# Experts stage: tokens and the list of indices read from PSUM, and the gathered rows spread anew

## What is computed

```python
q = (hb @ wq).reshape(128, 8, 2, 128)            # 8 heads, two halves
s = einsum('thsd,snd->thsn', q, subkeys)         # 128 keys for each half
s1, i1 = top_k(s[:, :, 0], 16);  s2, i2 = top_k(s[:, :, 1], 16)
sc, ci = top_k(s1[..., :, None] + s2[..., None, :], 16)
idx  = e1 * 128 + e2                             # of 16384 experts
gate = softmax(sc)
act  = gelu(einsum('td,thkd->thk', hb, u_tab[idx])) * gate
out  = einsum('thk,thkd->td', act, v_tab[idx])   # 128 choices for each token
```

## Time and profile before

| what | value |
|---|---|
| median of 3 runs | 4457.77 us (4456.28 to 4461.15) |
| span of the profiled execution | 4448.2 us |
| choice of the experts, units 0 to 75 | about 1027 to 1376 us |
| gates | about 1376 to 1638 us |
| last 14 units of the first table | to about 1702 us |
| second table | to about 2240 us |
| PE, DVE, ACT, POOL busy over the span | 95%, 70%, 41%, 35% |

### The profile page before, as it was taken

One profiled execution on the slowest core, in us unless ns is written; L12 is line 12 of the kernel. 1 busy time (PEld: TensorE's weight loads), 2 busy tenths in 40 slices (PEclk: granted clock), 3 DMA queues, 4 the chain that ended last, 5 costly groups with the idle time before them and its releaser, 6 DMA issues.

```text
span 4448.2 us, 66516 instructions
## 1 busy us (share of the span) xinstructions
PE 4243.8 (95%) x26227; PEld 3699.9 (83%) x26227; DVE 3101.9 (70%) x4740; ACT 1806.5 (41%) x2814; POOL 1550.2 (35%) x1005
## 2 busy tenths in 40 slices
PE   7979989999989999999999999999999999999998
PEld 5857745779989999999989877699889877877997
DVE  5866667559878988788878555588478544555873
ACT  4245411233334544333345335455255333323542
POOL 2044224215887657777721110211111110112121
PEclk8989999999999999999999999999999999999999
DMA  4133522224875779999933322133323332102332
GB/s 180 53 105 124 182 69 70 80 89 157 260 247 199 271 287 393 376 382 388 366 108 105 95 87 66 48 105 96 100 91 105 95 104 77 47 34 68 103 99 75
DMA packets 232190, 665.74 MB, mean 150 GB/s; under 512 B 22519, under 2 KB 88455, under 8 KB 229704
## 3 DMA queue, kind: packets, MB, share of 16 engines
q1 hardware_dynamic: 110528, 389.87, 26.1%
q0 software_dynamic: 38752, 142.90, 8.8%
q10 hardware_dynamic: 82600, 128.71, 8.1%
HBM read 593.24 MB, written 68.16 MB: 149 GB/s over the span
## 4 chain that ended last, share of the span: by engine, by line
PE 74%; DVE 16%; POOL 3%; ACT 3%; issue 3%; DMA 1%; ACTq 0%; DVEq 0%; POOLq 0%
PE ps L271 14%; PE ps L272 14%; PE ps L273 14%; PE ps L2727 5%; PE ps L2729 5%; PE ps L2728 5%; DVE r L240 2%; PE ps L1611 2%; DVE A L2042 2%; PE ps L3762 1%; PE ps L1690 1%; DVE A L2341 1%; POOL r L240 1%; DVE A L2342 1%; DVE r L290 1%
## 5 line engine op out<-in xcount | busy, mean ns | idle before, releaser
L271 PE MATMUL ps<-r,r 128*128 128x384 f32 (+1 forms) x3944 | 1454.4, 369 | 22.2 <-POOL r L240 14.6
L272 PE MATMUL ps<-r,r 128*128 128x384 f32 (+1 forms) x3944 | 1436.3, 364 | 0.0
L273 PE MATMUL ps<-r,r 128*128 128x384 f32 (+1 forms) x3944 | 1435.8, 364 | 0.0
L240 DVE TENSOR_TENSOR r<-A,r 128x1024 fp32r<-128x1024 f32 x436 | 603.9, 1387 | 718.7 <-ACT r L234 713.0
L234 ACT ACTIVATE r<-A 128x1024 fp32r<-128x1024 f32 x513 | 542.2, 1058 | 1200.9 <-PE ps L273 995.3
L271 PEld LDWEIGHTS ps<-r,r 128*128 128x128 f32 x3944 | 745.6, 189 | 118.7 <-issue 24.5
L272 PEld LDWEIGHTS ps<-r,r 128*128 128x128 f32 x3944 | 745.7, 189 | 81.5 <-issue 3.4
L273 PEld LDWEIGHTS ps<-r,r 128*128 128x128 f32 x3944 | 745.2, 189 | 81.6
L287 ACT ACTIVATE r<-A 128x512 fp32r<-128x512 f32 (+1 forms) x796 | 474.1, 611 | 503.4 <-DVE A L2415 233.5
L2727 PE MATMUL ps<-r,r 128*128 128x256 f32 x2128 | 601.0, 282 | 3.5 <-DVE A L2891 2.5
L2729 PE MATMUL ps<-r,r 128*128 128x256 f32 x2128 | 600.4, 282 | 0.0
(11 more groups left out here) (532 smaller groups left out, 5544.8 us busy)
## 6 DMA issues: line engine op xcount, KB each, us to landing
A<-in_pu SPq DMA_DIRECT2D x128, 512.0 KB
A<-in_pv SPq DMA_DIRECT2D x128, 512.0 KB
A<-in_f1i SPq DMA_DIRECT2D x88, 512.0 KB, 3.5
A<-in_f2i SPq DMA_DIRECT2D x88, 512.0 KB, 3.6
A<-in_w_in SPq DMA_DIRECT2D x48, 512.0 KB
acts<-A ACTq DMA_DIRECT2D x128, 192.0 KB
gates<-A ACTq DMA_DIRECT2D x8, 3072.0 KB, 11.3
A<-gates ACTq DMA_DIRECT2D x32, 768.0 KB
```

The source lines that it names most:

```text
L240: e.tensor_tensor(self.vr(at + 1024, 1024), self.v(self.st0 + 1024 * (u % RS), 1024), self.vr(at, 1024).bitcast(F32), ALU.subtract).then_i ...
L271: t.matmul(o, hi, xh, start=first and k == k0, stop=False)
L272: t.matmul(o, hi, xl, start=False, stop=False)
L273: m = t.matmul(o, lo, xh, start=False, stop=final and k == K - 1)
```

## The change

The last two banks become one tensor of 128 x 1024. It keeps the tokens' values, which PE wrote there by its transposes; rows of the first table numbered below `L.kept` (108) are multiplied with these in place of the copy `L.XT` in SBUF. The comparisons of `hot_v` read the list of indices from bank 2, where ACT copies it at unit 70. For that the units from 70 on use banks 0 and 1 in turn, and "gate t" moves from banks 6 and 7 to banks 3, 4 and 5, with a wait for the last scores. PE waits at x = 6 until row 107 is used, since "vsum" 6 overwrites the tokens. The rows of the first table are now 48, 40, 14 and 26 (in 20 groups) in place of 48, 28, 14 and 38 (in 28).

```diff
--- before.py
+++ after.py
@@ -111,7 +111,9 @@
         self.at0 = (nc.sbuf_base + 63) // 64 * 64
         self.A = nc.alloc_sbuf_tensor_at("A", [128, self.size], F32, offset=self.at0)
         self.rounded = {}
-        self.PS = [ctx.enter_context(nc.psum_tensor(f"ps{i}", [128, 512], F32)) for i in range(8)]
+        self.PS = [ctx.enter_context(nc.psum_tensor(f"ps{i}", [128, 512], F32)) for i in range(6)]
+        self.last2 = ctx.enter_context(nc.psum_tensor("ps67", [128, 1024], F32))
+        self.PS += [self.last2[:, 0:512], self.last2[:, 512:1024]]
         self.top = 0
         self.st0 = self.al(1024 * RS)
         self.wr0 = self.al(2048 * RW)
@@ -1981,6 +1983,7 @@
 
     def lay_peer(self):
         L = self.L3 = Area()
+        L.THREE = 70
         L.HN = self.HR
         self.top = L.HN + 8192
         L.XT, L.ROWS, L.ACC = self.al(1024), self.al(6144), self.al(1024)
@@ -2001,21 +2004,25 @@
         L.GB, L.AC, L.TM = self.al(12 * NT), self.al(32 * NT), self.HX
         self.plan([("q", o) for o in range(16)], range(4))
         self.plan([("scores", n) for n in range(16)], (4, 5))
+        L.bank = [c % 3 if c < L.THREE else (c + 1) % 2 for c in range(128)]
         for b in range(3):
-            self.plan([("early", c) for c in range(b, 128, 3)] + [("vsum", b)] + ([("sum t", b)] if b < 2 else []), (b,))
-            self.plan([("gates", i) for i in range(b, NT // 4, 3)] + [("vsum", 3 + b)], (3 + b,))
-        self.plan([("x tokens", 0), ("gate t", 1), ("gate t", 3), ("vsum", 6)], (6,))
-        self.plan([("x tokens", 1), ("gate t", 2), ("vsum", 7)], (7,))
+            self.plan([("early", c) for c in range(128) if L.bank[c] == b] + [("vsum", b)] + ([("sum t", b)] if b < 2 else []), (b,))
+        for b in range(3):
+            self.plan([("gate t", b + 1)] + [("gates", i) for i in range(b, NT // 4, 3)] + [("vsum", 3 + b)], (3 + b,))
+        for i in range(2):
+            self.plan([("x tokens", i)], (6 + i,))
+            self.plan([("vsum", 6 + i)], (6 + i,))
         L.norm = (4, 5, 6, 3)
 
 
         L.steps, n = {}, 0
-        for at, m in ([(("choices", i), 16 * (i + 1) // 3) for i in range(9)] + [(("gates", i), 48 + 28 * (i + 1) // 96) for i in range(96)]
-                      + [(("later", r), 76 + r + 1) for r in range(LATER)]
-                      + [(("second", x), min(90 + 38 * (x + 1) // 28, 128) if x < 30 else 128 + min(128, 128 * (x - 29) // 95)) for x in range(128)]):
+        for at, m in ([(("choices", i), 16 * (i + 1) // 3) for i in range(9)] + [(("gates", i), 48 + 40 * (i + 1) // 96) for i in range(96)]
+                      + [(("later", r), 88 + r + 1) for r in range(LATER)]
+                      + [(("second", x), min(102 + 26 * (x + 1) // 20, 128) if x < 30 else 128 + min(128, 128 * (x - 29) // 95)) for x in range(128)]):
             L.steps[at] = range(n, m)
             n = m
         assert n == 256
+        L.kept = L.steps["second", 4].stop
 
 
 
@@ -2039,7 +2046,8 @@
             row, c = self.v(L.ROWS + 1024 * (n % 6), 1024), n % 128
             v.wait_ge(*S.at("row", n))
             if n < 128:
-                v.scalar_tensor_tensor(out=row, in0=row, scalar=1.0, in1=self.v(L.XT, 1024), op0=ALU.mult, op1=ALU.mult,
+                tokens = self.last2[:, :] if n < L.kept else self.v(L.XT, 1024)
+                v.scalar_tensor_tensor(out=row, in0=row, scalar=1.0, in1=tokens, op0=ALU.mult, op1=ALU.mult,
                                        accum_out=self.v(L.DOT + c, 1)).then_inc(*S.on("v", "row used", n))
                 continue
             acc, w = self.v(L.ACC, 1024), self.v(L.COEF + c, 1)
@@ -2140,6 +2148,7 @@
             self.early_t(t, c)
             if c in self.TURN:
                 tt = self.TURN[c]
+                t.wait_ge(*S.at("out", "scores", 15))
                 ps = self.bank_t(t, "gate t", tt)
                 t.wait_ge(*S.at("gate", tt))
                 for i in range(3):
@@ -2167,6 +2176,9 @@
             if c < 4:
                 self.scores_a(a, 12 + c)
             self.early_a(a, c)
+            if c == L.THREE:
+                a.wait_ge(*S.at("out", "early", c - 2))
+                a.activation(self.PS[2][:, 0:128], self.cst("iota128"), ACT.Copy).then_inc(*S.on("a", "iota kept"))
             if c in self.EXP:
                 a.wait_ge(*S.at("below", self.EXP[c]))
                 a.activation(gg, gg, ACT.Exp).then_inc(*S.on("a", "gate exp", self.EXP[c]))
@@ -2334,7 +2346,7 @@
     def hot_v(self, v, b):
         S = self.S
         if b < NT // 8:
-            io = self.cst("iota128").unsqueeze(1).to_broadcast([128, 8, 128])
+            io = self.PS[2][:, 0:128].unsqueeze(1).to_broadcast([128, 8, 128])
             a, h, e1, e2, gate = self.one_hot(b)
             if b >= 4:
                 v.wait_ge(*S.at("gate mm", 2 * b - 7))
@@ -2350,6 +2362,7 @@
 
     def gates_v(self, v):
         S, L = self.S, self.L3
+        v.wait_ge(*S.at("iota kept"))
         v.wait_ge(*S.at("out", "gate t", 3))
         v.wait_ge(*S.last("v"))
         for b in range(3):
@@ -2449,6 +2462,8 @@
         for x in range(128):
             st, j = divmod(x, 8)
             ps = self.bank_t(t, "vsum", j) if st == 0 else self.ps("vsum", j)
+            if x == 6:
+                t.wait_ge(*S.at("row used", L.kept - 1))
             if x == 126:
                 t.wait_ge(*S.at("row used", 255))
                 for i in range(2):
```

## The result

The changed kernel took 4429.51 us (median of four runs, 4423.71 to 4434.17), the kernel before, run beside it, 4457.02 us (4451.72 to 4461.15). The ratio is 0.9935, with an interval of 0.9919 to 0.9951: faster, by about 28 us where 18.8 were forecast. The time forecast was 4439.0; the ratio on the 4457.8 us of before gives 4428.8, just under 4429, the lower end of the range.

A forecast was written before the change was run, and what follows sets the result against it. PE was taken as the bound, with room only in its pauses before and in the gates, where DVE and POOL hold each other. Terms -9 - 1.6 - 1.7 - 8.4 + 0.3 + 1.6 = -18.8 us: 4457.8 to 4439.0; range 4429 to 4449.

The forecast's parts named there:

- (c): Before the gates: eight PE pauses, 9.5 us in all, ending wide two-tensor operations in SBUF; half, 5 us, taken as gain.
- (5): New bank plan: 0.3 us lost to late Gelus, plus a new 1.6 us wait at the second table's first group.
- Rival B: Operand in PSUM frees nothing; twelve more rows cost a full DVE 18 us in the gates: 4478 us, chance 0.05.
- (1): Rows beside units 14 to 75, before the gates: shorter gathers and low parts shrink fourteen PE pauses, gaining 9 us.
- (2): Start of the gates: unheld last low part and first product take 1.6 us off the 7.25 us of waiting.
- (a): Before the gates: three pauses behind a gather awaiting DVE's first row of a block; 0.84 us each, 2.5 us gained.
- (3): Soon after the gates start: the 1.72 us pause goes through shorter gathers and third product, gaining 1.7 us.
- (4): Rest of the gates: DVE needs 227 us, under PE's 245.8, so the other 8.4 us of pauses go.
- rival A: DVE stays the bound in the gates, its low parts still taking 2.63 us: 4447 us, chance 0.12.
- C: Gathers stay at 1.76 us beside a row, so most pauses before the gates remain: 4447 us, chance 0.05.
- D: All eight pauses of sort (c) go and PE's clock doesn't halve after shorter pauses: 4431 us, chance 0.12.
- E: Transfers for twelve more rows in the gates delay weights or Gelu, losing 4 to 10 us: 4446 us, chance 0.08.

The follow-up runs named there:

- e1: Changed kernel with rows and comparisons both reading SBUF again, banks and new row spread kept: 4479.85 us, ratio 1.0041 to the kernel before.
- e8: Changed kernel with the edits of e5, e6 and e7 together: 4412.11 us, ratio 0.9903 to the kernel before.
- e9: e8 with POOL's third product also moved ahead of its four gathers: 4416.05 us, ratio 0.9904 to the kernel before.
- e5: Changed kernel with units from 69 on in banks c mod 2, so unit 127 leaves bank 0: 4433.45 us, ratio 0.9947 to the kernel before.
- e6: Changed kernel with POOL's first two products queued behind the low parts of units 73 and 74: 4423.34 us, ratio 0.9933 to the kernel before.
- e2: Changed kernel with only the comparisons reading PSUM, tokens from SBUF, rows spread as before: 4442.58 us, ratio 0.9966 to the kernel before.
- e4: Changed kernel with both operands in PSUM but rows spread as before: 4429.26 us, ratio 0.9934 to the kernel before.
- e7: Changed kernel with ACT's last three exponentials, and PE's transposes, three units earlier: 4423.97 us, ratio 0.9924 to the kernel before.
- e10: Changed kernel run again unedited, in the same rounds as e9: 4434.13 us, ratio 0.9948 to the kernel before.
- e3: Changed kernel with only the rows reading tokens from PSUM, comparisons from SBUF, rows spread as before: 4435.54 us, ratio 0.9954 to the kernel before.

## Where the prediction was right, and where its sum was too small

The mechanism came as forecast, and the time ended just under the range, because the gain was too small in three terms of the sum. The pauses of sort (c) were taken at half and went nearly whole (3.0 us). What a pause costs beside its marked idle was put at 1 us before the gates, where it is 4.1, and at nothing in the gates, where it is 3.6. The net cost of (5) came out 1.2 us smaller, by a spacing of units that the prediction doesn't have.

**Does an operand in PSUM end the holding.** Right, on the strength of 76 instances in the earlier trace rows that belonged to another form: the 108 rows and the comparisons stand at 1.20 to 1.23 us to the last one. Rival B is refuted by after and its price shown by e1, with 13.4 us in the gates where 18 were worked out. (Its point of decision, given as 4.8 us of extra work, is 4.6: 256 - 251.4.) Reading from PSUM cost nothing: 1.212 us at the median against 1.219 from A. The fixed costs in the Trainium skill (VectorE: DVE Perf Modes, "The TRN2 errata"), from which the prediction estimated 0.065 us more for each, aren't borne out here, as the prediction took it.

**(1) and (2), 10.6 forecast, 16.7 measured.** Of the 17.8 us marked 6.7 are left, where the forecast leaves 9.8. (a) is as said, with the longest pause at 4.70: the gather now takes 0.95 and the low part 2.37, with DVE's rows beside it at 1.21 (timeline of after):

```profile
1254.61 0.95 POOL L2036 DMA_INDIRECT A<-in_u_rows,A  x1 [9.79 <-DVE A L2050]
1255.57 2.37 POOL L242 TENSOR_TENSOR r<-A,r 128x1024 fp32r<-128x1024 f32 x1
...
1258.09 0.42 PE L273 MATMUL ps<-r,r 128*128 128x384 f32 x1 [4.70 <-POOL r L242]
```

The other five marks add up to 2.05 us, so of the 9.5 us of (c) at least 7.4 went. I had taken half, 5, and my own working of one stretch, 2.2 to 3.2 of 3.9, pointed higher. The start of the gates went from 7.25 to 5.68, the 1.6 of step (2). With it the marks lost 12.6 us, 3.0 more than forecast. The second term that was mis-sized is the last of (1): a pause "also costs PE some 0.15 us that isn't counted as idle: 1 us". It is 4.1. In before, the first of the long pauses reads so, and behind it a delay that has no mark:

```profile
1153.13 0.34 PE L273 MATMUL ps<-r,r 128*128 128x384 f32 x1
1154.39 0.42 PE L271 MATMUL ps<-r,r 128*128 128x384 f32 x1 [0.93 <-POOL r L240]
1154.65 0.34 PE L272 MATMUL ps<-r,r 128*128 128x384 f32 x1
1154.82 0.34 PE L273 MATMUL ps<-r,r 128*128 128x384 f32 x1
...
1181.24 0.34 PE L273 MATMUL ps<-r,r 128*128 128x384 f32 x1
1181.61 0.41 PE L271 MATMUL ps<-r,r 128*128 128x384 f32 x1
```

Matmuls of this shape follow one another every 0.176 us though each is shown 0.34 long, so that 0.17 us of every pause lie under the matmul before it; and the one after the pause is followed in 0.26, 0.08 later than usual. Each pause costs about 0.25 us more than its mark. Eight marks fewer make 2.0 us of the 4.1. Five delays of some 0.19 us with no mark at all, in before (the row at 1181.61 is one, 0.37 behind the last), each with the same 0.08 after it, make 1.4 more. The rest is the clock. Behind the longest pause PE is at the half clock from 1263.11 to about 1268.2 in before, 5.1 us, and for 3.4 in after; half of the difference, 0.8 us, is lost. A stretch of before, and one of after in which the clock is full again:

```profile
1263.00:1268.00 5.00, 4.89 (x15) 4.92 (x16) 5.00 (x5) 0.00 (x0) 4.71 (x3) 0.50 0.86 267
```

```profile
1262.00:1264.00 2.00, 2.00 (x13) 2.00 (x13) 1.97 (x3) 0.00 (x0) 2.00 (x1) 1.00 0.82 258
```

The better reading would have been by the floor: 67 units at 4.224 us and 1 us are 284.0, and before took 315.8, 31.8 over it, where the marks add up to 25.0. e8, with no pause, took 283.74.

**(3) and (4), 10.1 forecast, 13.7 measured.** The mechanism holds in each part. L2361 is unheld, and L242 on DVE came down by 1.15 us (DVE by line in the gates, 1371 to 1612 us; the earlier trace rows has it at 2631):

```profile
L242 DVE TENSOR_TENSOR r<-A,r 128x1024 fp32r<-128x1024 f32 x37 | 54.8, 1482 | 43.0 <-ACT r L236 43.0
```

It had been put at 1.9, where rival A wanted 2.63 with 2.4 as the point of decision. It is well under both. DVE now waits for ACT's high part before it (43 us of idle, all in front of this line), so that it starts when PE lets it and not when the comparison ends; that it meets fewer products for this reason is argued, not tested. DVE was to need 227 us and needs 197.5. What failed is the price of the pauses. The forecast took off the idle that the trace marks, 1.7 and 8.4 us, and 10.2 us of marked idle went. The stage lost 13.7: 1.6 more beside the seven pauses (as above, 0.23 for each), 1.7 in delays between matmuls that have no mark, and 0.2 of the half clock at the start. The prediction's floor should have shown it and didn't, because it was miscounted: (4) has 96 groups and 38 units in 245.8 us, but only 37 units lie in the stretch that it was held against. From the first pair to the start of the last it is 94 x 0.89 + 37 x 4.22 = 239.8 us, and e9 took 239.88. So the room in before was 15.4 us, where the prediction saw 11.4 and thought it nearly all marked. What is left, 1.6 against e9, is PE at the half clock behind the pause at the start: 3.2 us of work at it, from 1367.87 to about 1371.

**(5), 1.9 forecast, 0.7 measured.** The pause came at the place and with the size forecast (1.58 us marked, on the Gelu of unit 127), and e5 removed it by the bank alone. The 0.3 for two banks came at the place named, where ACT is late: after has no mark there, but a delay of 0.2 us behind ACT's Gelu (near 1640.8), e6 and e1 have a marked wait of 0.18 and 0.26, and e2, e4, e7 and e10 none. So both parts of the step were about right, some 2.0 us in all. The stage is 1.2 us better than the 1.9 for no reason of the step: unit spacing, 4.224 in before and 4.213 in after, 128 times.

**(6) and (7), nothing.** So it was: no wait at x = 6, none at the transposes, and e4 has the twelve rows at nothing.

**The frame.** The prediction, and the part on the profile before it, let 9.6 us lie around the span. It is 1.8 in every run, so the 9.6 were mostly the difference between one execution and the median of the others. Taken from the span the forecast would have been 4448.2 - 18.8 + 1.8 = 4431.2, for an execution like the profiled one; it can't be leant on, with runs of one kernel 10 us apart. The range was too narrow by the terms above, not by the noise alone: its lower end is 28.8 us off, and the stages lost 29.8. Of these 29.8 us, 11.0 are over the 18.8: 3.0 are (c), 3.1 what pauses cost beside their marks before the gates, 3.6 the same in the gates, 0.0 step (2), and 1.2 the spacing of the table's units.

**The other rivals.** C is refuted (gathers at 0.975 at the median; in after, up to the end of the gates, only those beside an operation with both tensors in A are long, 2.8 us at the wide ones and 1.8 at L242, and none beside a row). The remark of the Trainium skill (SBUF — State Buffer, "Who interferes with whom") behind it, marked there as inferred, isn't borne out as the prediction took it, since the gathers were held by two-input operations and are no longer. But each gather also reads its row numbers from A, and no run tells whether it is held at that or at making its descriptors. D was right about the pauses of sort (c), nearly all of which went, and wrong about the clock, which still fell after the pause at the gates (0.58 in the stretch 1363 to 1371 above). E: the DMA share rose from 0.71 to 0.83 in the gates and nothing came late. So it took none of the gain in these stages.

## What to carry to other kernels

In this kernel, where DVE and POOL both ran operations on two tensors in SBUF, one stood still for the other's whole instruction. One operand that is read over and over (tokens, a list of indices), put into a spare PSUM bank, freed both engines, and the one that wasn't changed gained too: POOL's product went from 2.81 to 1.90 us. Price what is taken off a bound stage by the stage's length over its floor (units counted in that very stretch, times their spacing), not by the idle time that the trace marks: the marks fell by 12.6 and 10.2 us, the stages by 16.7 and 13.7. And look where a stage has room before work is moved into it: with DVE full the move went with 13 us more in the gates, with room made first it cost nothing.

## What was not expected of the hardware

The marked idle of PE is low by about 0.25 us for each pause, delays of 0.19 us get no mark at all, and the half clock behind a pause comes on top, as worked out above. And the clock behind a pause isn't told by the pause's length alone: after 5.68 us (after) and 4.70 us of idle the granted clock was 0.50 to 0.54 for a few microseconds (1.2 GHz), and after the same pause of 2.7 us at the same place it was 0.50 in e8 and 1.00 in e6. The gates of e8 are longer than those of e6 by 1.6 us, which is that. What decides it no run shows; e8 had PE without a pause from unit 8 up to there, e6 had six marked ones.

The units of the second table follow one another at 4.224 us in before, e1, e3, e5, e6 and e8 and at 4.213 in after, e2, e4, e7, e9 and e10. It repeats where one kernel was run twice (after and e10), and goes with neither the bank, the operands, the rows nor the pause. It is worth 1.4 us over the table, and its cause is open.
